# The last tile of a mixture-of-experts combine: its scaled rows and first pick formed on GpSimd, added on TensorE by an identity product

## The reference

```python
h = layer_norm(ALPHA * x + merged @ w_out, ln1_g, ln1_b)
# hier_moe: the gates of a token are weights[n] at its two picked experts, else 0
acc + g[:, None] * ((jax.nn.silu(a) * b) @ wd)        # summed over the experts
return layer_norm(ALPHA * h + f, ln2_g, ln2_b)        # f is that sum
```

## Time and profile before

| what | value |
|---|---|
| median of three runs | 1185.95 us (1184.62 to 1187.92) |
| the profiled execution | 1185.41 us |
| its span | 1183.6 us |
| PE busy | 1155.5 us, 98% |
| DVE busy | 740.1 us, 63% |
| ACT busy | 596.9 us, 50% |
| POOL busy | 87.1 us, 7% |
| mean granted TensorE clock | 0.996 of full speed |

### The profile page before, as it was taken

How to read it: one execution, slowest core, us unless ns; L and a number is a source line. 1 busy time by engine, 2 the same in 40 slices (tenths; PEclk the granted TensorE clock), 3 DMA queues, 4 the chain that set the end, 5 groups by cost and what they waited for, 6 DMA issues and landing times. The chain is left out here.

```text
span 1183.6 us, 20345 instructions
## 1 busy us (share of the span) xinstructions
PE 1155.5 (98%) x7145; PEld 1024.0 (87%) x7145; DVE 740.1 (63%) x1353; ACT 596.9 (50%) x1007; POOL 87.1 (7%) x91
## 2 busy tenths in 40 slices
PE   9999999999999999999989999899999999999997
PEld 8999999899999999999979899788788888878862
DVE  3326355365454653646555765557899999889945
ACT  3233343433444334343465733303688888788852
POOL 0000000000000000000000000011222222222113
PEclk9999999999999999999999999999999999999999
DMA  6623425325252153522523335723799999999916
GB/s 203 169 78 106 113 64 154 92 63 144 72 151 76 53 154 88 140 83 59 162 73 107 90 103 177 257 90 119 290 359 362 362 355 372 373 357 367 363 51 265
DMA packets 178475, 210.50 MB, mean 178 GB/s; under 512 B 14054, under 2 KB 141543, under 8 KB 178428
## 3 DMA queue, kind: packets, MB, share of 16 engines
q1 hardware_dynamic: 155440, 188.07, 48.0%
q10 hardware_dynamic: 13644, 10.77, 2.9%
q0 software_dynamic: 9344, 11.03, 2.7%
HBM read 200.19 MB, written 32.71 MB: 197 GB/s over the span
## 5 line engine op out<-in xcount | busy, mean ns | idle before, releaser
L349 PE MATMUL bank_u<-x_hi,w_hi 128*128 128x320 f32 (+1 forms) x1024 | 326.6, 319 | 0.4 <-DVE x_lo L786 0.4
L350 PE MATMUL bank_u<-x_lo,w_hi 128*128 128x320 f32 (+1 forms) x1024 | 318.9, 311 | 0.0
L351 PE MATMUL bank_u<-x_hi,w_lo 128*128 128x320 f32 (+1 forms) x1024 | 318.0, 311 | 0.0
L349 PEld LDWEIGHTS bank_u<-x_hi,w_hi 128*128 128x128 f32 x1024 | 192.5, 188 | 8.6 <-issue 7.1
L350 PEld LDWEIGHTS bank_u<-x_lo,w_hi 128*128 128x128 f32 x1024 | 192.9, 188 | 0.0
L351 PEld LDWEIGHTS bank_u<-x_hi,w_lo 128*128 128x128 f32 x1024 | 192.7, 188 | 0.0
L781 DVE TENSOR_TENSOR w_lo<-w_raw,w_hi 128x1024 fp32r<-128x1024 f32 x80 | 97.8, 1222 | 114.7 <-ACT w_hi L552 114.0
L552 ACT CAST w_hi<-w_raw 128x1024 fp32r<-128x1024 f32 x80 | 83.5, 1043 | 45.6 <-issue 28.4
L1548 PE MATMUL banks<-w_hi_space,xT_hi 128*128 128x512 f32 x256 | 102.6, 401 | 1.2 <-issue 1.2
L1550 PE MATMUL banks<-w_hi_space,xT_lo 128*128 128x512 f32 x256 | 99.9, 390 | 0.0
L1549 PE MATMUL banks<-w_lo_space,xT_hi 128*128 128x512 f32 x256 | 99.8, 390 | 0.0
(11 more groups left out here) (294 smaller groups left out, 2170.4 us busy)
## 6 DMA issues: line engine op xcount, KB each, us to landing
w_raw<-in_w_in SPq DMA_DIRECT2D x64, 512.0 KB, 4.1
first_up<-in_w_gate_up SPq DMA_DIRECT2D x16, 2048.0 KB, 12.3
second_up<-in_w_gate_up SPq DMA_DIRECT2D x16, 2048.0 KB, 12.4
first_down<-in_w_down SPq DMA_DIRECT2D x16, 1024.0 KB, 11.2
second_down<-in_w_down SPq DMA_DIRECT2D x16, 1024.0 KB, 11.0
k_cache<-in_cache_k SPq DMA_DIRECT2D x16, 512.0 KB
v_cache<-in_cache_v SPq DMA_DIRECT2D x16, 512.0 KB
w_raw<-in_w_branch SPq DMA_DIRECT2D x16, 512.0 KB, 4.4
```

The lines of the kernel that those rows point to most:

```text
L349: pe.matmul(out, w_hi[:, u % 2, k, :], x_hi[:, k, cols], start=(k == 0), stop=False)
L350: pe.matmul(out, w_hi[:, u % 2, k, :], x_lo[:, k, cols], start=False, stop=False)
L351: last = pe.matmul(out, w_lo[:, u % 2, k, :], x_hi[:, k, cols], start=False, stop=(k == KT - 1))
```

## The change

For tile 4 alone the sum is made in another way. POOL multiplies `h[:, LAST]` by ALPHA in place, as its first work in `combine` (a `tensor_scalar` on 128x1024). Between its additions of `ln_b` for tile 0 and for tile 1 it waits for the first pick of tile 4, multiplies it by the weights in place (another `tensor_scalar`, with a scalar for each partition), drains, adds the scaled `h` (a `tensor_tensor`) and raises a new semaphore, `first_added`. PE no longer issues the residual products and the products with `diag[:, LAST, 0]`. It issues those with the second pick for both halves first, then waits for `first_added`, then adds POOL's result by two products with the identity matrix, one for each half, which raise `summed`.

```diff
+        first_added = sem("first_added")
+        ident = keep["const"][:, C_ID:C_ID + P]
...
                 if b >= 4:
 
                     pe.wait_ge(taken, b - 3)
-                    residual(pe, b)
+                    pe.wait_ge(picked_in[b][1], 16)
+                    for cols in halves:
+                        pe.matmul(bank_y[b % 4][:, cols], diag[:, b, 1, :], picked[:, b, 1, cols], start=True, stop=True, skip_group_check=True)
+                    pe.wait_ge(first_added, 1)
+                    for cols in halves:
+                        pe.matmul(bank_y[b % 4][:, cols], ident, picked[:, b, 0, cols], start=False, stop=True, skip_group_check=True).then_inc(summed, 1)
+                    continue
...
         def gpsimd(g):
+            g.tensor_scalar(h[:, LAST, :], h[:, LAST, :], ALPHA, None, ALU.mult)
             g.wait_ge(small_in, 32)
             for b in range(LAST):
                 y = picked[:, b, 0, :]
+                if b == 1:
+                    first = picked[:, LAST, 0, :]
+                    g.wait_ge(picked_in[LAST][0], 16)
+                    g.tensor_scalar(first, first, keep["weights"][:, 0, LAST:TB], None, ALU.mult)
+                    g.drain()
+                    g.tensor_tensor(first, first, h[:, LAST, :], ALU.add).then_inc(first_added, 1)
                 g.wait_ge(rescaled, b + 1)
                 g.tensor_tensor(y, y, ln_b, ALU.add).then_inc(y_ready, 1)
```

## The result

The changed kernel took 1192.07 us, the median of 11 runs (1188.72 to 1193.49). Beside them the kernel before took 1184.78 (11 runs, 1183.05 to 1187.92). The ratio is 1.0056, with a 95% interval of 1.0047 to 1.0065: about 6.6 us slower. The forecast was 1186.0, with a range up to 1188.6; its scale was the median of three runs, 1.2 us above that of the eleven. The span of the profiled execution went from 1183.6 to 1190.4 us, so the profiles show the difference too, 6.8 us.

The account below looks back on a forecast made before the run. PE was taken to bound the tail; its 1.72 us saving was taken up by waiting for POOL's tile 3 and three transfers at once, net 0.0 us, so 1186.0 us on the median's scale, range 1183.8 to 1188.6.

Parts of the forecast that it names:

- PE's part: PE, tile 4: 8 records removed, 4 added, so 1.72 us less on PE and the chain through DVE 1.72 us earlier.
- part 2: POOL's new work: h scaled in idle time, multiplication (1.4 us), drain (0.05), addition (2.35); sum ready at 1172.1, before PE asks.
- t: Duration of POOL's multiplication of tile 4's first pick, a 1024-column TENSOR_SCALAR, taken as 1.4 us, likely between 0.9 and 2.35.
- The sum: End of the kernel: PE's 1.72 us taken up by waiting for POOL's tile 3 and three transfers; net 0.0 us.
- the queue behind POOL: POOL's additions for tiles 1 to 3, 2.35 us each, run back to back; tile 3 ends at 1179.3, 1.3 us later.
- the stores in order: SP's queue: tile 4's stores stand behind tile 3's; landing takes 2.6 plus 1.25 us, last at 1183.2 against 1183.16.
- The reading of the end: Last 31 us: PE bounds the tail, and each microsecond off its tile 4 shortens the end if nothing else is late.
- Quick POOL: Rival on POOL's multiplication: t near 0.9, part of PE's gain comes through, 0.5 to at most 1.72 us; chance 0.22.
- The point from which PE waits: PE in tile 4 waits for POOL's sum (first_added) only if t is above 2.9 us.
- Slow POOL that collides with DVE: Rival: t 2.35 makes the end 1.0 us later, or 2.5 if tile 3's addition waits for DVE's L1850; chance 0.18.
- Very slow POOL: Rival: TENSOR_SCALAR at the 32-column rate, 15.5 us, end 16 us later; t from 5.0 costs over 3.6; chance 0.05.
- The chance of 0.07 for slower: Whole kernel: slower by more than 3.6 us, needing t above 5 or a worse collision than worked out; chance 0.07.

Follow-up runs that it names:

- e3_pe_only: Kernel before with only PE's change: PE adds tile 4's first pick as it lies, scaled h and that pick's weight left out; 1185.00 us, ratio 0.9999.
- e4_act: Changed kernel with tile 4's first-pick multiplication moved to ACT, POOL's addition moved behind its tile 1, no drain between; 1184.99 us, ratio 1.0002.
- e6_act_drain: e4_act with one more POOL drain, in idle time at the start of combine, behind the scaling of h; 1183.80 us, ratio 0.9992.
- e7_early_drain: Changed kernel with one more POOL drain in idle time at the start of combine, the change's own drain kept; 1185.41 us, ratio 1.0010.
- e1_sem: Changed kernel with POOL's drain between tile 4's multiplication and addition replaced by a semaphore that POOL raises and waits for; 1187.18 us, ratio 1.0015.
- e10_before_drain: Kernel before with one POOL drain at the start of combine, behind the last scatter, and nothing else; 1184.58 us, ratio 1.0002.
- e9_pe_only_drain: e3_pe_only with one more POOL drain in idle time at the start of combine; 1183.68 us, ratio 0.9990.

## Why the prediction was wrong

**PE's part was right.** Four records less, 1.72 us, and DVE's chain 1.7 us shorter: `e3_pe_only` shows both, and in the changed kernel the second pick's products start at 1171.78 without a wait.

**The step that failed** is in part 2: "After a short drain (0.05, as between DVE's rows, an estimate)". It was 5.30, because POOL's first drain behind 64 indirect DMAs pays for them all, which the prediction had nowhere. A drain on one engine was priced by rows of another, while a row of the right engine was in the trace: POOL's closing drain, 5.32 us behind its last addition. As it lies between the multiplication and `first_added`, all that POOL does afterwards was later by it.

**A term was mis-sized**: t was taken as 1.4 us and measured 2.84. Of the bounds given, 0.9 and 2.35, even the upper was too low; only the far one from the 32-column row held it. The choice rested on counting streams (one in, one out, like a MEMSET), and that doesn't order POOL's instructions: COPY 1.03, TENSOR_TENSOR 1.88 and 2.35, TENSOR_SCALAR 2.79. The Trainium skill (GPSIMD Engine Reference, Engine selection) calls one-input work roughly line-rate. The copy agrees with it; TENSOR_SCALAR, at 2.56 ns a column, does not, and the measurement decides.

**The sum, with the two put right**, comes out: 0.0 + (2.84 - 1.4) + (5.30 - 0.05) = 6.7 us, against 6.8 in the profiles. So the rest of the working held: the queue behind POOL, the stores in order, and 3.9 us from the end of tile 3's addition to the last landing (4.0 in the changed kernel, 4.0 in `e4_act`, `e6_act_drain` and `e7_early_drain`).

**The reading of the end was wrong, but by luck at no cost in the sum.** "So PE bounds the tail, and each microsecond taken from PE's tile 4 would be one from the end, if nothing else is late" left out a second path that ended within 0.2 us of the last store, POOL's closing drain. It is why `e3_pe_only` and `e4_act` gained nothing. In the changed kernel it cost nothing only because the drain inside the change had been long instead (the closing one ends 0.08 us behind POOL). The rival *Quick POOL* could not have come about either: with t at 0.9, the 5.3 us stand ahead of tile 3's addition or, with a semaphore in place of the drain, behind it, at 1178.8 + 5.3 = 1184.1 (worked out, not run).

**The rivals.** The point from which PE waits, t above 2.9, was nearly reached by t alone, and passed with the drain. "Slow POOL that collides with DVE" foresaw the lock. It shows in `e1_sem`: tile 3's addition runs from 1176.36 to 1178.71, and the two L1865 (the old L1850) that start at 1176.70 take 3.22 us instead of 1.41 for the pair in the earlier trace rows.

```profile
1176.70 3.22 DVE L1865 SCALAR_TENSOR_TENSOR picked<-picked,small,ya 128x512 f32<-128x512 f32 x2
```

The first of them is held until POOL is done (1178.71 - 1176.70 = 2.0, close to the 1.8 us in excess). That is as the Trainium skill has it (SBUF — State Buffer, Who interferes with whom), with POOL as the first comer. As worked out, it didn't move the end: in `e7_early_drain`, which shows the lock too (3.25 us for the pair) and has a short closing drain, the last landing is 4.0 us behind POOL's tile 3, and so it is in `e4_act` and `e6_act_drain`, where the pair takes 1.4. "Very slow POOL" came nearest in what followed: it said that from t = 5.0 on the end is more than 3.6 us later. The time between the starts of the multiplication and the addition was 8.2 us. But it had that for t alone, and t was 2.84. The chance of 0.07 for slower was too small because the drain had been given no range at all.

## What to carry to other kernels

Ask the trace what a drain costs on that engine, by the drain rows of its own line, and look at the closing drains before taking the last store for the end. On POOL, when the kernel issues many indirect DMAs, put a drain where POOL is idle behind the last of them, or keep a same-engine dependence in order by a semaphore; the semaphore alone leaves the cost to the closing drain, as in `e1_sem`. Two paths that end within 0.2 us of each other hide each other's gains: `e3_pe_only` (one path shortened) and `e10_before_drain` (the other) gain nothing, and both together (`e9_pe_only_drain`) gain 1.2 us.

## What the runs showed of the hardware

- A drain on POOL, all DMAs landed, ends behind POOL's work by 83 to 85 ns for each indirect DMA (of 128 rows) issued since the last drain: 2.37 us for 28, 5.32 for 64, 0.04 without any. The next drain is short (0.1 us). What POOL does in that time no run shows.
- On POOL, 128x1024 float32: COPY 1.03 us, MEMSET 0.94, TENSOR_TENSOR with a broadcast column 1.88, with two full inputs 2.35, TENSOR_SCALAR 2.79 to 2.84 (512 columns 1.48).
- After an idle stretch of 5.46 us PE's next four records ran at the lower clock, 3.78 us instead of 1.88.
